# Attention values of the late steps as 64-by-64 products in three rounds, turning moved behind the scores, and each score minimum signalled by itself

## The chip, the cores and the metric

The kernel runs on one core of a Trainium2 chip. The metric is the device time of one execution in microseconds (us); less is better. The engines are named as in the profile: PE is TensorE (PEld its weight loads), DVE is VectorE, ACT is ScalarE, POOL is GpSimd, SP is SyncE, which here only issues DMAs. Each engine works through its own queue in order, and waits in it on semaphores.

## The reference, cut to what matters

One step of a two-layer decoder trunk on 1,024 prompt tokens and 8 sample tokens, 1,024 features wide, in fp32. Layer 0 is a gated linear recurrence. Layer 1 is attention with 16 query heads of 64 features and 2 key/value heads, over a window of 128 keys, with a learned sink for each head, and a SiLU gate on its output. The change touches the attention of the prompt alone:

```python
def _sink_attention(q, k, v, mask, sinks):
    s = jnp.einsum('bnqkgd,bnskd->bnkgqs', q, k) * scale      # blocks of 128 queries by 256 keys
    s = jnp.where(valid, s, MASK_VALUE)                       # 0 <= query - key <= 128
    m = jnp.maximum(jnp.max(s, axis=-1, keepdims=True), sink)
    p = jnp.where(valid, jnp.exp(s - m), 0.0)
    denom = jnp.sum(p, axis=-1, keepdims=True) + jnp.exp(sink - m)
    return jnp.einsum('bnkgqs,bnskd->bnqkgd', p / denom, v)
```

The result is multiplied by the gate and goes through a product with `w_out`, a residual add and a last RMS norm.

## The kernel before, in words

Weights and activations of the large products are cut into a high and a low part (fp32r), and each product is three passes (high by high, high by low, low by high); every such matmul streams 344 tokens. They fill PE for nearly the whole kernel. The attention is spread over that stream of matmuls as **steps**, `for s in range(-3, NQ)` with `NQ` = 32. Query group `q` (0 to 31) is four heads of one block of 128 queries: `q // 8` picks the heads, `q % 8` the block. Where `q % 8` is 0 there is no block of keys in front, and each piece of work for that q is half as large. In step s PE does, in this order:

- `values(s - 1)`: probabilities times values. It waits until both turned halves of the probabilities have been copied to SBUF (`pt_early` by ACT, `pt_late` by DVE) and until the output before it has been read (`gated`).
- `turn(s)`: transposes the probabilities of s into two PSUM banks, after POOL's `normalise(s)` (`p_done`). It signals `pt_done`.
- `scores(s + 2)`: queries by keys, in quarters of 64 features by 64 queries, after the minima of s + 1 have been read (`sc_read`). It signals `sc_done`.
- its share of the large products: 16 or 17 matmuls in a step (`gates_part`) up to s = 15, and 18 in a step (`output_part`) from s = 16 on. Output unit 0 of token segment i waits for `tile_lo` of that segment.

`two_banks(q)` is true for q from 11 (`Q_TWO`) on, other than q = 16 and 24: 19 of the 32 groups. There `values` uses two PSUM banks, `R[4]` for the first 64 queries and `G[2]` for the other 64, and leaves out the keys that the window masks: first four products of 128 keys by 64 features (the "far" ones), then four of 64 keys by 64 features (the "near" ones). For other q there are four products of 128 keys by 64 features over 256 columns, half as many where `q % 8` is 0. An fp32 matmul shows as two MATMUL records.

In step s DVE does `denominators(s + 1)` (waits for the exponentials of s + 1), `gate_output(s - 1)` (waits for `pv_done`), `copy_late(s)` (waits for `pt_done`), `minima(s + 2)` (four reductions from PSUM, waits for the scores and for `turn(s)`, whose buffer it writes), and then the **extra work** that the step has: evacuating gate units (`gate_raw2`, `gate_minimum`) or output units (`first_half`), low parts of weights (`prepare`, `prepare_half`), small pieces for the sample tokens, and in s = 15, 16, 17 the low part of a token segment (`AR`, "tile_lo"). ACT does `copy_early(s)`, from s = 17 on `cut_slice(s - 1)`, then high parts, the three functions of a gate's softplus, and last `exponentials(s + 2)`, which waits until all four minima have been taken. POOL does `normalise(s + 1)` after DVE's `denominators(s + 1)`.

Of the kernel before, what the change touches and what calls it, by code (L numbers as in the profile page):

```python
# [126 lines left out]
def output_fill(s):  # L127

    return 18 * max(0, s - 15)


GATE_END = [min(s for s in range(-3, NQ) if gates_fill(s) >= 24 * (g + 1)) for g in range(NU * (HP - BG_FIRST))]
OUT_END = [min(s for s in range(NQ) if output_fill(s) >= 12 * (g + 1)) for g in range(NU * KT)]
SLOT = (2, 3, 4, 5, 0, 1, 6, 7)


# [18 lines left out]
def build(nc, ctx, ins, outs):  # L155
# [234 lines left out]
    rd_done = sem("rd_done")  # L390
    p_done = sem("p_done")
    pt_done = sem("pt_done")
    pt_early = sem("pt_early")
    pt_late = sem("pt_late")
    pv_done = sem("pv_done")
# [26 lines left out]
    def seg(i):  # L422
        return slice(i * TU, (i + 1) * TU)
# [465 lines left out]
    def _(act):  # L889
# [276 lines left out]

        def exponentials(q):
            keys = slice(P if q % NC == 0 else 0, 2 * P)
            act.wait_ge(sc_read, 2 * q + 2)
            sm = small[:, q % 2]  # L1170
            for i in range(4):
                nc.scalar.activation(SP_[q % 2][:, i, keys], SP_[q % 2][:, i, keys], ACT.Exp, bias=sm[:, 0, i:i + 1],  # L1172
                                     scale=-1.0, accum_out=sm[:, 2, i:i + 1])
            act.wait_ge(m_ready, q + 1)
            nc.scalar.activation(sm[:, 3, :], sm[:, 1, :], ACT.Exp).then_inc(p_exp, 1)
# [15 lines left out]
        for s in range(-3, NQ + 1):  # L1191
            if 0 <= s < NQ:
                copy_early(s)
            if s >= 17:
                cut_slice(s - 1)
            for n in range(N_B2 + 2, N_BO):
                if end_step(n - 3) + 1 == s:
                    prepare(n)
            for h in range(2 * KT):
                if half_step(h) == s:  # L1200
                    prepare_half(h)
            if s == 5:
                act.wait_ge(d_max, 1)
                nc.scalar.activation(SSN[:], SSN[:], ACT.Exp, bias=dsm[:, 1:2], accum_out=dsm[:, 3:4])
                nc.scalar.activation(dsm[:, 4:5], dsm[:, 2:3], ACT.Exp).then_inc(d_exp, 1)
            if 15 <= s < 18:
                i = s - 15
                act.wait_ge(unit_done, NU * (N_BO - 1) + i + 1)
                act.wait_ge(gated, (11, 14, 16)[i])
                act.wait_ge(d_gated, 1)  # L1210
                nc.scalar.activation(XL[:, 0:HK, seg(i)], A[:, 0:HK, seg(i)], ACT.Copy).then_inc(tile_hi, 1)
            if s == 22:
                act.wait_ge(d_gated, 2)
                nc.scalar.activation(XL[:, HK:HP, SEQ:T], A[:, HK:HP, SEQ:T], ACT.Copy).then_inc(dec_hi, 1)
            for g in range(NU * (HP - BG_FIRST)):
                if GATE_END[g] + 2 == s:
                    gate_exponential(NU * BG_FIRST + g)
            for g in range(NU * (HP - BG_FIRST)):
                if GATE_END[g] + 1 == s:
                    gate_softplus(N_B2 + g // NU, g % NU)  # L1220
            if 0 <= s + 2 < NQ:
                exponentials(s + 2)
# [34 lines left out]
    def _(dve):  # L1257
# [384 lines left out]
        def minima(q):  # L1642

            keys = slice(P if q % NC == 0 else 0, 2 * P)
            sm = small[:, q % 2]
            h = 4 * (q // NC)
            if q >= 2:
                dve.wait_ge(pt_done, q - 1)
            for jj in range(2):
                dve.wait_ge(sc_done, 2 * q + 2)  # L1650
                for v in range(2):
                    i = 2 * jj + v
                    ps = R[v][:, 2 * P * jj:2 * P * (jj + 1)]
                    ins = nc.vector.tensor_tensor_reduce(  # L1654
                        out=SP_[q % 2][:, i, keys], in0=ps[:, keys], in1=amask[:, keys], scale=1.0,
                        scalar=sink[:, h + i:h + i + 1], op0=ALU.add, op1=ALU.min, accum_out=sm[:, 0, i:i + 1])
                ins.then_inc(sc_read, 1)
            dve.wait_ge(sc_read, 2 * q + 2)
            nc.vector.tensor_tensor(sm[:, 1, :], sm[:, 0, :], sink[:, h:h + 4], ALU.subtract).then_inc(m_ready, 1)

        def denominators(q):
# [51 lines left out]
        for s in range(-3, NQ + 1):  # L1713
            if 0 <= s + 1 < NQ:
                denominators(s + 1)
            if 0 <= s - 1:
                gate_output(s - 1)
            if 0 <= s < NQ:
                copy_late(s)
            if 0 <= s + 2 < NQ:  # L1720
                minima(s + 2)
            for g in range(NU * (HP - BG_FIRST)):
                if GATE_END[g] == s:
                    gate_raw2(N_B2 + g // NU, g % NU)
# [42 lines left out]
                                      ).then_inc(d_done, 1)  # L1767
            if s == 14:
                sample_gates(0, HK, 1)
            if 15 <= s < 18:  # L1770
                i = s - 15
                dve.wait_ge(tile_hi, i + 1)
                nc.vector.tensor_tensor(AR[:, 0:HK, seg(i)], A[:, 0:HK, seg(i)], XL[:, 0:HK, seg(i)].bitcast(fp32),  # L1773
                                        ALU.subtract).then_inc(tile_lo, 1)
            if s == 21:
                sample_gates(HK, HP, 2)
            if s == 22:
# [19 lines left out]
    def _(pe):  # L1797
# [280 lines left out]
        def scores(q):  # L2078
            p, nb = query(q)
            keys = slice(P if nb == 0 else 0, 2 * P)  # L2080
            tok = slice((nb - 1) * P + keys.start, (nb + 1) * P)
            if q:
                pe.wait_ge(sc_read, 2 * q)
            else:
                pe.wait_ge(q_rot, HP)
                pe.wait_ge(kb_done, 1)
            for jj in range(2):
                for v in range(2):
                    rows = slice(64 * v, 64 * v + 64)
                    if nb == 0:  # L2090
                        ins = nc.tensor.matmul(R[v][:, 2 * P * jj + P:2 * P * (jj + 1)], pair(A, q)[rows, jj],
                                               KNEG[rows, tok], start=True, stop=True)
                        continue
                    for u in range(0, P, 64):
                        ins = nc.tensor.matmul(R[v][u:u + 64, 2 * P * jj + u:2 * P * jj + u + 192],  # L2095
                                               pair(A, q)[rows, jj, u:u + 64],
                                               KNEG[rows, tok.start + u:tok.start + u + 192], start=True, stop=True)
                ins.then_inc(sc_done, 1)

        def turn(q):  # L2100
# [9 lines left out]
                                                  ident[rows, rows])  # L2110
            ins.then_inc(pt_done, 1)

        def values(q):
            p, nb = query(q)
            pe.wait_ge(pt_early, q + 1)
            pe.wait_ge(pt_late, q + 1)
            if q:
                pe.wait_ge(gated, q)
            blocks = key_blocks(q)
            if two_banks(q):  # L2120
                if q == Q_TWO:
                    pe.wait_ge(d_done, 1)
                for near in range(2):
                    for u in range(2):
                        kb = u ^ near
                        ks = slice(64 * kb ^ 64, (64 * kb ^ 64) + 64) if near else slice(0, P)
                        for v in range(2):
                            rows = slice(64 * v, 64 * v + 64)
                            ins = nc.tensor.matmul(  # L2129
                                (R[4], G[2])[u][rows, 0:P].rearrange("p (j w) -> p j w", j=2),  # L2130
                                VP[ks, nb - 1 + kb, rows],
                                turned(kb)[ks, :, v, u],
                                start=not near, stop=bool(near))
                ins.then_inc(pv_done, 1)
                return
            for kb in blocks:
                for v in range(2):
                    rows = slice(64 * v, 64 * v + 64)
                    ins = nc.tensor.matmul(R[4][rows, 0:2 * P].rearrange("p (j u w) -> p j u w", j=2, u=2),  # L2139
                                           VP[:, nb - 1 + kb, rows], turned(kb)[:, :, v], start=(kb == blocks[0]), stop=(kb == 1))  # L2140
            ins.then_inc(pv_done, 1)
# [44 lines left out]
        for s in range(-3, NQ):  # L2186
            if s >= 1:
                values(s - 1)
            if s >= 0:
                turn(s)  # L2190
            if s == 0:
                pe.wait_ge(vp_done, 2)
            if 0 <= s + 2 < NQ:
                scores(s + 2)
            if s < 16:
                gates_part(gates_fill(s - 1) if s > -3 else 0, gates_fill(s))
            else:
                output_part(output_fill(s - 1), output_fill(s))
# [17 lines left out]
            if s == 9:  # L2216
# [6 lines left out]
                                           stop=(b == DEC - 1))  # L2223
                ins.then_inc(d_out, 1)
        values(NQ - 1)
        pe.wait_ge(dec_lo, 1)
        for i, ready in enumerate((11, 14, 16)):
            pe.wait_ge(slice_lo, ready)
# [82 lines left out]
```

## Time and profile before

| | |
|---|---|
| time, median of 3 (lowest to highest) | 954.62 us (953.82 to 955.58) |
| the profiled execution: its own time / its span | 955.42 us / 953.5 us |
| PE busy | 942.5 us of the span, 99% |
| DVE / ACT / POOL busy | 608.2 / 409.9 / 396.3 us |
| steps of the attention | scores from 712 us on, last values at 896 us |
| DMA | 89.86 MB in all, 93 GB/s over the span |

The span is from the first to the last instruction of the profiled execution; the own time has some 1.9 us more around it. A record's start is exact enough to take the pace of an engine from the distance of two starts; the length of a matmul record holds its latency too, so that lengths of neighbouring records overlap.

### The profile page before, as it was taken

How to read it: one execution, taken by the hardware profiler on the slowest of the kernel's cores; microseconds unless marked ns; L12 is line 12 of the kernel's file. 1: busy time of each engine (PE TensorE's matmuls, PEld its weight loads, DVE VectorE, ACT ScalarE, POOL GpSimd, SP SyncE). 2: the span in 40 equal slices, each digit the busy share in tenths (PEclk: the TensorE clock that was granted, in tenths of full speed). 3: DMA queues.
4: the chain of work that ended last, by engine and by line, in shares of the span. 5: the costliest groups of instructions: out<-in, count | busy, mean ns of one | idle time of the engine just before them, and what ended most of it. 6: DMA issues, size and time to landing. Idle time of an engine off the chain costs nothing.

```text
span 953.5 us, 21616 instructions
## 1 busy us (share of the span) xinstructions
PE 942.5 (99%) x8948; PEld 895.0 (94%) x8948; DVE 608.2 (64%) x1220; ACT 409.9 (43%) x821; POOL 396.3 (42%) x295
## 2 busy tenths in 40 slices
PE   9999999999999999999999999999999999999996
PEld 9999999999999999899999999999998788788995
DVE  6596676767575666639733235466667877977634
ACT  7532424243434334434422233532127768766423
POOL 2383635445362734403234441451105534445343
PEclk9999999999999999999999999999999999999999
DMA  9422121313131304334033413221112223333104
GB/s 356 184 91 80 58 101 59 93 46 94 45 93 46 114 25 138 113 105 149 23 134 138 151 67 134 73 90 45 45 54 88 68 68 111 98 92 88 34 31 149
DMA packets 53202, 89.86 MB, mean 94 GB/s; under 512 B 15625, under 2 KB 35049, under 8 KB 52977
## 3 DMA queue, kind: packets, MB, share of 16 engines
q1 hardware_dynamic: 52672, 88.11, 27.7%
q8 instruction: 71, 1.16, 0.5%
q10 hardware_dynamic: 432, 0.37, 0.1%
q14 instruction: 27, 0.21, 0.1%
HBM read 70.83 MB, written 17.64 MB: 93 GB/s over the span
## 4 chain that ended last, share of the span: by engine, by line
PE 94%; DMA 2%; SPq 1%; ACT 1%; DVE 1%; issue 0%; POOL 0%; DVEq 0%; ACTq 0%
PE G L1820 66%; PE G L2164 9%; PE R L2095 2%; PE R L2109 2%; DMA ST<-xs 2%; PE R L1933 1%; PE R L1921 1%; PE R L2129 1%; PE R L1891 1%; PE R L1936 1%; PE R L1820 1%; PE R L2139 1%; PE R L1861 1%; PE R L1911 1%; SPq L547 1%; PE R L1873 1%
## 5 line engine op out<-in xcount | busy, mean ns | idle before, releaser
L1820 PE MATMUL G<-XH,WH 128*128 128x344 f32 x1152 | 370.5, 324 | 0.6 <-ACT XH L1021 0.6
L1820 PE MATMUL G<-XL,WH 128*128 128x344 f32 x1152 | 366.9, 321 | 0.0
L1820 PE MATMUL G<-XH,WL 128*128 128x344 f32 x744 | 234.0, 320 | 0.1
L1820 PEld LDWEIGHTS G<-XH,WH 128*128 128x128 f32 x1152 | 216.0, 188 | 7.7 <-issue 5.2
L1820 PEld LDWEIGHTS G<-XL,WH 128*128 128x128 f32 x1152 | 216.0, 188 | 2.5 <-issue 2.2
L741 POOL TENSOR_TENSOR WL<-WR,WH 128x1024 fp32r<-128x1024 f32 x40 | 107.5, 2687 | 188.7 <-ACT WH L908 162.1
L1820 PEld LDWEIGHTS G<-XH,WL 128*128 128x128 f32 x744 | 139.1, 188 | 0.4 <-POOL WL L741 0.4
L1820 PE MATMUL G<-XL,WL 128*128 128x344 f32 x408 | 130.7, 320 | 0.0
L840 POOL TENSOR_TENSOR SP<-SP,small 128x1024 f32<-128x1024 f32 (+1 forms) x32 | 57.2, 1789 | 115.4 <-DVE small L1665 115.4
L908 ACT ACTIVATE WH<-WR 128x1024 fp32r<-128x1024 f32 x56 | 59.0, 1055 | 57.3 <-PE G L1820 30.8
L779 POOL TENSOR_TENSOR K<-K,FP 128x512 f32<-128x512 f32 x48 | 61.3, 1277 | 48.5 <-PE R L1911 14.1
L1820 PEld LDWEIGHTS G<-XL,WL 128*128 128x128 f32 x408 | 76.7, 188 | 0.8 <-issue 0.6
L1172 ACT ACTIVATE SP<-SP,small 128x256 f32<-128x256 f32 (+1 forms) x128 | 61.7, 483 | 32.3 <-DVE small L1654 32.3
L735 POOL TENSOR_TENSOR WR<-WR,gain 128x1024 f32<-128x1024 f32 x18 | 37.0, 2064 | 60.2 <-DMA WR<-w 60.2
L1820 PE MATMUL G<-AR,WH 128*128 128x344 f32 x192 | 61.3, 319 | 0.0
L1820 PE MATMUL G<-GR,WH 128*128 128x344 f32 x192 | 61.3, 319 | 0.0
L1820 PE MATMUL G<-GR,WL 128*128 128x344 f32 x192 | 61.3, 319 | 0.0
L1654 DVE CUSTOM_DVE_ANT_0 SP<-R,amask,sink 128x256 f32<-128x256 f32 (+1 forms) x128 | 52.0, 462 | 3.7 <-PE R L2095 3.3
L2164 PE MATMUL G<-XL,WH 128*128 128x344 f32 x144 | 48.0, 333 | 0.4 <-DVE AR L1773 0.4
L2164 PE MATMUL G<-XL,WL 128*128 128x344 f32 x144 | 46.0, 319 | 0.0
L2164 PE MATMUL G<-AR,WH 128*128 128x344 f32 x144 | 45.9, 319 | 0.0
L1553 DVE TENSOR_TENSOR H<-G,RESO 128x344 f32<-128x344 f32 x24 | 12.3, 514 | 40.4 <-PE G L1820 40.2
(303 smaller groups left out, 1779.1 us busy)
## 6 DMA issues: line engine op xcount, KB each, us to landing
WR<-w SPq DMA_DIRECT2D x56, 512.0 KB, 3.9
A<-x SPq DMA_DIRECT2D x8, 516.0 KB, 7.7
FG<-head_scales SPq DMA_DIRECT2D x8, 516.0 KB, 3.7
RESO<-x SPq DMA_DIRECT2D x8, 516.0 KB, 4.6
h_spill<-H SPq DMA_DIRECT2D x8, 516.0 KB, 2.9
gate_spill<-EV SPq DMA_DIRECT2D x24, 172.0 KB, 1.9
RES<-h_spill SPq DMA_DIRECT2D x24, 172.0 KB, 2.6
SS<-states SPq DMA_DIRECT2D x8, 512.0 KB, 5.8
```

Source lines behind the costliest of these rows:

```text
L735: nc.gpsimd.tensor_tensor(WR[:, n % 3], WR[:, n % 3], gain[:, kind, :].unsqueeze(2).broadcast_to([P, KT, P]), ALU.mult).then_inc(gained, 1)
L741: nc.gpsimd.tensor_tensor(WL[:, n % 3], WR[:, n % 3], WH[:, n % 3].bitcast(fp32), ALU.subtract).then_inc(lo_pool, 1)
L779: nc.gpsimd.tensor_tensor(low, low, decay(l, 1).unsqueeze(2).broadcast_to([P, SEQ // (2 * h), h]), ALU.mult).then_inc(upd_k, 1)
L840: nc.gpsimd.tensor_tensor(sp_, sp_, small[:, q % 2, 4, :].unsqueeze(2).broadcast_to([P, 4, keys.stop - keys.start]), ALU.mult).then_inc(p_ ...
L908: nc.scalar.activation(WH[:, n % 3], WR[:, n % 3], ACT.Copy).then_inc(hi_done, 1)
L1172: nc.scalar.activation(SP_[q % 2][:, i, keys], SP_[q % 2][:, i, keys], ACT.Exp, bias=sm[:, 0, i:i + 1], scale=-1.0, accum_out=sm[:, 2, i:i ...
L1553: nc.vector.tensor_tensor(H1[:, m, seg(i)], G[i][:, 0:TU], RESO[m % 2][:, seg(i)], ALU.add).then_inc(unit_read, 1)
L1654: ins = nc.vector.tensor_tensor_reduce(out=SP_[q % 2][:, i, keys], in0=ps[:, keys], in1=amask[:, keys], scale=1.0, scalar=sink[:, h + i:h ...
L1820: return nc.tensor.matmul(U[unit_bank(NU * n + i)][:, 0:TU], w[:, n % 3, k, :], x[:, seg(i)], start=(k == 0 and p == 0), stop=(k == KT - 1 ...
L2095: ins = nc.tensor.matmul(R[v][u:u + 64, 2 * P * jj + u:2 * P * jj + u + 192], pair(A, q)[rows, jj, u:u + 64], KNEG[rows, tok.start + u:tok ...
L2109: ins = nc.tensor.transpose(R[2 + u][:, cols], SP_[q % 2][rows, i, kb * P:(kb + 1) * P], ident[rows, rows])
L2164: return nc.tensor.matmul(G[unit_bank(u)][:, 0:TU], wt[:, k, :], x, start=(w == 0), stop=(w == 11))
```

## The change

The values of a two-bank group become twelve products of 64 keys by 64 features in three rounds of four. Rounds 1 and 2 stand where `values` stood, the scores of s + 2 come next, then round 3 (`rest_values`), and `turn(s)` is last. Round 3 writes the two banks from the other half of the array's rows, and waits for the end of round 2 on a new semaphore, `pv_most`. The other groups keep their products, but `turn(s)` comes behind `scores(s + 2)` for them too. On DVE `minima(s + 2)` goes ahead of `copy_late(s)`. `sc_read` is raised by each of the four minima, and ACT takes each exponential after its own minimum. The three segment low parts (with ACT's high parts) go from steps 15, 16, 17 to 15, 18, 22, and on DVE to right behind `copy_late`.

```diff
+TILE_STEP = (15, 18, 22)
...
         def exponentials(q):
             keys = slice(P if q % NC == 0 else 0, 2 * P)
-            act.wait_ge(sc_read, 2 * q + 2)
             sm = small[:, q % 2]
             for i in range(4):
+                act.wait_ge(sc_read, 4 * q + i + 1)
                 nc.scalar.activation(SP_[q % 2][:, i, keys], SP_[q % 2][:, i, keys], ACT.Exp, bias=sm[:, 0, i:i + 1],
...
-            if 15 <= s < 18:
-                i = s - 15
+            if s in TILE_STEP:
+                i = TILE_STEP.index(s)
...
-                    ins = nc.vector.tensor_tensor_reduce(
+                    nc.vector.tensor_tensor_reduce(
...
-                ins.then_inc(sc_read, 1)
-            dve.wait_ge(sc_read, 2 * q + 2)
+                        ).then_inc(sc_read, 1)
+            dve.wait_ge(sc_read, 4 * q + 4)
...
+            if 0 <= s + 2 < NQ:
+                minima(s + 2)
             if 0 <= s < NQ:
                 copy_late(s)
-            if 0 <= s + 2 < NQ:
-                minima(s + 2)
+            if s in TILE_STEP:
+                i = TILE_STEP.index(s)
+                dve.wait_ge(tile_hi, i + 1)
+                nc.vector.tensor_tensor(AR[:, 0:HK, seg(i)], A[:, 0:HK, seg(i)], XL[:, 0:HK, seg(i)].bitcast(fp32),
+                                        ALU.subtract).then_inc(tile_lo, 1)
...
-            if 15 <= s < 18:
-                i = s - 15
-                dve.wait_ge(tile_hi, i + 1)
-                nc.vector.tensor_tensor(AR[:, 0:HK, seg(i)], A[:, 0:HK, seg(i)], XL[:, 0:HK, seg(i)].bitcast(fp32),
-                                        ALU.subtract).then_inc(tile_lo, 1)
...
-                pe.wait_ge(sc_read, 2 * q)
+                pe.wait_ge(sc_read, 4 * q)
...
+        def quarter_values(q, n, *parts):
+
+            nb = query(q)[1]
+            for u, (kb, kh) in enumerate(parts):
+                ks = slice(64 * kh, 64 * kh + 64)
+                for v in range(2):
+                    rows = slice(64 * v, 64 * v + 64)
+                    ins = nc.tensor.matmul((R[4], G[2])[u][rows, 0:P].rearrange("p (j w) -> p j w", j=2),
+                                           VP[ks, nb - 1 + kb, rows], turned(kb)[ks, :, v, u], start=(n == 0), stop=(n == 2))
+            return ins
+
+        def rest_values(q):
+
+            if two_banks(q):
+                pe.wait_ge(pv_most, sum(two_banks(v) for v in range(q + 1)))
+                quarter_values(q, 2, (0, 1), (1, 0)).then_inc(pv_done, 1)
...
             if two_banks(q):
                 if q == Q_TWO:
                     pe.wait_ge(d_done, 1)
-                for near in range(2):
-                    for u in range(2):
-                        kb = u ^ near
-                        ks = slice(64 * kb ^ 64, (64 * kb ^ 64) + 64) if near else slice(0, P)
-                        for v in range(2):
-                            rows = slice(64 * v, 64 * v + 64)
-                            ins = nc.tensor.matmul(
-                                (R[4], G[2])[u][rows, 0:P].rearrange("p (j w) -> p j w", j=2),
-                                VP[ks, nb - 1 + kb, rows],
-                                turned(kb)[ks, :, v, u],
-                                start=not near, stop=bool(near))
-                ins.then_inc(pv_done, 1)
+                quarter_values(q, 0, (0, 0), (0, 1))
+                quarter_values(q, 1, (1, 0), (1, 1)).then_inc(pv_most, 1)
                 return
...
             if s >= 1:
                 values(s - 1)
-            if s >= 0:
-                turn(s)
             if s == 0:
                 pe.wait_ge(vp_done, 2)
             if 0 <= s + 2 < NQ:
                 scores(s + 2)
+            if s >= 1:
+                rest_values(s - 1)
+            if s >= 0:
+                turn(s)
...
         values(NQ - 1)
+        rest_values(NQ - 1)
```

## Rows read from the trace of the kernel before

**Rows 1.** The page: the span, and each engine's busy time.

```profile
span 953.5 us, 21616 instructions
PE 942.5 (99%) x8948; PEld 895.0 (94%) x8948; DVE 608.2 (64%) x1220; ACT 409.9 (43%) x821; POOL 396.3 (42%) x295
```

**Rows 2.** Waits from 722 to 900 us: who waited, for whom, total, times, longest.

```profile
DVE small L1664 <- ACT small L1175: 24.4, 25, 1.6
...
PE R L2129 <- DVE PT L1673: 0.5, 1, 0.5
```

**Rows 3.** Timeline of PE in a late step: start, us, engine, line, tiles, shapes.

```profile
864.75 0.32 PE L2164 MATMUL G<-XL,WXL 128*128 128x344 f32 x1
865.00 0.44 PE L2129 MATMUL R<-PT,VP 128*64 128x128 f32 x4
...
865.59 0.33 PE L2129 MATMUL R<-PT,VP 64*64 64x128 f32 x2
...
865.97 0.72 PE L2109 MATMUL R<-ident,SP 64*128 64x64 f32 x16
866.62 0.88 PE L2095 MATMUL R<-KNEG,A 64*64 64x192 f32 x16
867.43 0.43 PE L2164 MATMUL G<-XL,WXH 128*128 128x344 f32 x1
```

**Rows 4.** Timeline of PE, a step whose turning is half as large.

```profile
855.68 0.46 PE L2109 MATMUL R<-ident,SP 64*128 64x64 f32 x8
...
856.07 0.88 PE L2095 MATMUL R<-KNEG,A 64*64 64x192 f32 x16
```

**Rows 5.** Timeline of DVE around a late step, and ACT's copy behind turning.

```profile
868.02 0.48 DVE L1654 CUSTOM_DVE_ANT_0 SP<-R,amask,sink 128x256 f32<-128x256 f32 x1
...
869.84 0.52 DVE L1694 TENSOR_TENSOR H<-G,RES 128x344 f32<-128x344 f32 x1
...
871.96 0.16 DVE L1664 TENSOR_TENSOR small<-small 128x4 f32<-128x4 f32 x1 [1.61 <-ACT small L1175]
872.07 0.88 PE L2095 MATMUL R<-KNEG,A 64*64 64x192 f32 x16
...
872.18 0.60 ACT L1183 ACTIVATE PT<-R 128x512 f32<-128x512 f32 x1 [0.25 <-PE R L2109]
...
872.25 0.27 DVE L1682 TENSOR_TENSOR A<-R,SGR 128x128 f32<-128x128 f32 x1
...
872.64 0.68 DVE L1673 COPY PT<-R 128x512 f32<-128x512 f32 x1
```

**Rows 6.** Timeline of DVE and PE in steps 16 to 18, with PE's two waits.

```profile
813.33 0.43 PE L2164 MATMUL G<-XL,WH 128*128 128x344 f32 x1 [0.43 <-DVE AR L1773]
...
817.63 1.29 DVE L1265 TENSOR_TENSOR WL<-WR,WH 128x512 fp32r<-128x512 f32 x2
...
819.26 1.58 DVE L1773 TENSOR_TENSOR AR<-A,XL 128x1376 fp32r<-128x1376 f32 x1
...
821.29 0.32 PE L2164 MATMUL G<-XL,WL 128*128 128x344 f32 x1
...
821.37 0.68 DVE L1673 COPY PT<-R 128x512 f32<-128x512 f32 x1
...
822.15 0.44 PE L2129 MATMUL R<-PT,VP 128*64 128x128 f32 x4 [0.55 <-DVE PT L1673]
```

**Rows 7.** Timeline of DVE's extra work in step 4.

```profile
749.67 1.22 DVE L1260 TENSOR_TENSOR WL<-WR,WH 128x1024 fp32r<-128x1024 f32 x1
...
751.91 0.15 DVE L1664 TENSOR_TENSOR small<-small 128x4 f32<-128x4 f32 x1
```

**Rows 8.** Timeline of ACT and DVE in step 12.

```profile
792.01 1.14 ACT L920 ACTIVATE WH<-WR 128x512 fp32r<-128x512 f32 x2
...
793.06 0.48 ACT L1150 ACTIVATE EV<-EV 128x344 f32<-128x344 f32 x1
...
795.00 0.52 DVE L1609 SCALAR_TENSOR_TENSOR EV<-EV,EV 128x344 f32<-128x344 f32 x1 [0.44 <-ACT EV L1146]
```

More of the change, by code:

```diff
@@ L392, in build @@
     pt_done = sem("pt_done")
+    pv_most = sem("pv_most")
     pt_early = sem("pt_early")
@@ L1653, in minima @@
                     ps = R[v][:, 2 * P * jj:2 * P * (jj + 1)]
-                    ins = nc.vector.tensor_tensor_reduce(
+                    nc.vector.tensor_tensor_reduce(
                         out=SP_[q % 2][:, i, keys], in0=ps[:, keys], in1=amask[:, keys], scale=1.0,
-                        scalar=sink[:, h + i:h + i + 1], op0=ALU.add, op1=ALU.min, accum_out=sm[:, 0, i:i + 1])
-                ins.then_inc(sc_read, 1)
-            dve.wait_ge(sc_read, 2 * q + 2)
+                        scalar=sink[:, h + i:h + i + 1], op0=ALU.add, op1=ALU.min, accum_out=sm[:, 0, i:i + 1]
+                        ).then_inc(sc_read, 1)
+            dve.wait_ge(sc_read, 4 * q + 4)
             nc.vector.tensor_tensor(sm[:, 1, :], sm[:, 0, :], sink[:, h:h + 4], ALU.subtract).then_inc(m_ready, 1)
```

## The prediction

> **What bounds the kernel now.** I read the page first: PE is busy for 942.5 of 953.5 us [rows 1], so only what shortens or lengthens PE's own queue counts. Next the waits from 722 to 900 us, the stretch of the steps [rows 2]: PE hardly waits (0.5 us once, for DVE's late copy; the timeline shows 0.43 us more for a segment low part [rows 6]). DVE waits 24.4 us for ACT's exponentials. That costs nothing as long as PE does not wait for DVE in turn. Then the timeline of one late step. It shows what PE's step is made of, and that the parts hold fixed time besides their streaming.
>
> **PE's late step before** [rows 3]. The first values record starts at 865.00, the near ones at 865.59, turning at 865.97, scores at 866.62, the large products at 867.43. So values take 0.97 us, turning 0.65 us, scores 0.81 us. How much of a part is fixed? Turning with 8 records takes 0.39 us [rows 4], with 16 it takes 0.65 us [rows 3]: 8 records cost 0.26 us, and about 0.14 to 0.16 us is left over. The other parts fit the same. A round of the near products is four at a time; if a fp32 record of 128 columns takes 0.107 us on each of four quarters (scores have 192 columns and 4 rounds: 4 x 0.16 = 0.64 us of their 0.81), the near block is 2 x 0.107 + 0.17 = 0.38 us, as measured. The far block runs two at a time: 4 x 0.107 + 0.16 = 0.59 us, as measured. I take 0.16 us for each change of the array's shape (128x64, 64x64, 64x128, 128x128), and 0.09 us from the large products into values (864.75 + 0.157 to 865.00).
>
> The Trainium skill (TensorEngine Tiling (Array Packing), Key Properties) says that changing the tiling mode, and not merely the tile, drains the array. It gives no time for it; the sum would be the same by it, and it is the reason why I tie the 0.16 us to the change of shape and not to each part.
>
> **What the new form saves on PE.** Streaming is equal: before 4 far rounds and 2 near ones (0.43 + 0.21 us), after 6 rounds of 0.107 us, 0.64 us. Changes of shape: before far, near, turning, scores, large; after values/scores/round 3 all in 64x64, then turning, then large. Far to near is gone in all 19 two-bank groups: 19 x 0.16 = 3.0 us. Turning to scores is gone where scores still follow, 16 times: 16 x 0.16 = 2.6 us. Together 5.6 us. In the other steps the order changes and the count of shapes does not: 0.
>
> **The wait for `pv_most`.** The end of a part reaches another engine about 0.27 us after its streaming ends: ACT's copy starts 0.11 us after the block behind turning (872.07 to 872.18 [rows 5]), plus the 0.16 us before that block. With 0.08 us to get going again this is 0.35 us. Scores stream for 0.64 us in between, so it is hidden 16 times. In steps 30, 31 and after the last one no scores stand there: 3 x 0.35 = 1.05 us lost. Bounds: 0 and 0.5 us each.
>
> The Trainium skill (TensorE: Matmul & The Clock Gate, "The cost: per-tile semaphore tail") gives 25 + 4.7 x 4 + 26.3 = 70 ns as the tail of one signal behind four tiles. By that, as an estimate, the three waits would cost 0.2 us in place of 1.05 us; no row here shows a PE wait for itself.
>
> **The new hand-off.** A late step after the change, from the start of values: rounds 1 and 2 end at 0.43, scores at 1.07, round 3 at 1.28, turning runs from 1.44 to 1.93, large products start at 2.09 and take 17 x 0.157 + 0.20 = 2.86 (18: 3.03), so the next values could start at 4.95 to 5.12. Now DVE: `minima` needs turning, which is now last, and gets its signal at 2.20. Four minima take 1.62 and with the small subtraction 1.82 us (868.02 to 869.84 [rows 5]); only then comes `copy_late`, 0.68 us long, and PE starts 0.10 us after its end (821.37 + 0.68 to 822.15 [rows 6]). Values can start at 2.20 + 1.82 + 0.78 = 4.80. That leaves 0.15 to 0.3 us. Before, the copy came ahead of the minima and had 2.4 us to spare in this stretch. In an early step (values 1.01, scores 0.81, turning 0.65) the signal is at 2.57, the copy through at 5.17 and values due at 5.33: 0.16 us.
>
> So from DVE's end of the copy (4.60) to the next turning signal (4.95 + 2.20) there are 2.55 us, of which denominators take 0.29 and the output 0.40 us (871.96 to 872.25 to 872.64 [rows 5]). Extra work above some 1.9 us, or anything that holds the denominators, pushes minima, copy and then PE. I went through the 32 steps with the durations of the rows. Five overflow:
> - **Step 4**: two gate records (0.85), a whole weight low part and the sample tokens' chain (749.67 to 751.91, 2.24 us [rows 7]) make 3.1 us, with a short wait for ACT 3.4; room with slack is 2.5. PE waits 1.0 us in step 5.
> - **Step 12**: ACT has its copy, two weight halves (1.05, start to start [rows 8]), the exponential and a softplus (1.56) behind turning: 2.20 + 0.49 + 1.05 + 0.37 + 1.56 + 0.15 = 5.8, that is 0.86 into the next step. There DVE's `gate_minimum` waits (it waited 0.44 before [rows 8]), then 0.42 + 1.2 for the two low halves, 0.69, minima at 3.58 in place of 2.20, values at 6.16 in place of 4.97: 1.2 us.
> - **Step 15**: ACT's high part of the segment (1.24) stands in the same queue; its exponentials end at 2.9 of step 16, minima start at 3.77, PE waits 1.2 us.
> - **Step 16**: 0.42 + two low halves 1.2 + 0.43, after 0.3 of waiting: 0.5 us. **Step 18**: segment low part 1.5 (its record is 1.58 long [rows 6]) + 0.6 + 0.43: 0.5 us.
>
> Sum 4.4 us. The same addition over step 17 of before gives a wait of 0.75 us where the rows show 0.61 (822.15 against 821.29 + 0.157 + 0.09 = 821.54, [rows 6]), so I take a tenth off: 4.0 us.
>
> **Waits that go.** The segment low parts of before cost PE 0.5 us in step 16 (`AR`; the large products started at 813.33 [rows 6] where scores of 0.81 us would have let them start at 812.83), 0.61 us in step 18, and 0.25 us of small waits around: 1.4 us back. The moved ones are due in steps 16, 21 and 26, so none is late. Each minimum signalled alone: ACT starts its exponentials 1.2 us sooner, and DVE waits less for them (1.61 us in that step [rows 5]). PE is not behind that wait, so 0 by itself; where ACT's queue is the late one (steps 12, 15) it starts at once either way. SyncE's load of the gate waits for `gated`, now 0.5 us later, for data needed two steps on: 0. POOL's normalising has a step to spare: 0.
>
> **Sum**: -5.6 + 1.05 + 4.0 - 1.4 = -1.95 us, taken as -1.9. The profiled span 953.5 would become 951.6; its own time 955.42 lies 0.8 us above the median shown; against the median 954.62 I predict **952.7 us**. Own range: all of the five stalls in full and 0.5 us each for the last waits give about -1.1; none of the last waits and half of the stalls -5.0; -3.6 to -0.3 is where I see it.
>
> **Rivals.**
> - **The stalls do not come** (the slack of 0.15 us is larger, ACT is ahead): -5.6 + 1.05 - 1.4 = -6.0, at least -4: 948.6 to 950.6. For it: DVE waits for ACT in 25 steps before [rows 2], so it has time. Against: that time lies ahead of the denominators, not between turning and the copy. 0.18.
> - **The hand-off binds in ordinary steps**: if signals take 0.3 us more than I add, some 24 ordinary steps wait 0.15 us each: +3.6 - 1.9 = +1.7, 956.3. It decides from 0.25 us on. The slack is that thin. 0.14.
> - **Quarter products are slower than 0.107 us a round** (the side where it gets slower): only 8 records in a row at 64x64 and 128 columns are seen [rows 3], and the fixed part cannot be told from the pace there. At the pace of the scores, 0.04 us a record, 24 records take 0.96 and not 0.64 us: 19 x 0.32 = +6.1, 958.8. The gain is gone once a record takes 0.031 us in place of 0.027. 0.12. The Trainium skill (TensorEngine Tiling (Array Packing), Instruction Overhead) puts about 60 cycles on every matmul, so that more and smaller ones win nothing; 128 columns are above that, so by it the pace would hold.
> - **The change of shape costs nothing by itself**: the 0.16 us is the fill of any new block; then little of the 5.6 us comes and the stalls stay: +1 to +3.7, 955.6 to 958.3. Against: the near block shows 0.17 with the same banks, operands and line as the far one. 0.08.
>
> **Chances and range.** My forecast 0.48, half of it beyond 0.2% (1.9 us, which is about what a measurement of this kernel can tell from no change), half within. Faster by over 0.2%: 0.24 + 0.18 = 0.42. Within: 0.24 + 0.07 (thin hand-off) + 0.02 = 0.33. Slower: 0.07 + 0.10 + 0.08 = 0.25. The range leaves out the ends of the first and the third rival: 949.0 to 957.0; that of the forecast alone is 951.0 to 954.3.
>
> **What would show it.** In the trace after: no gap between rounds 2 and scores, the late step from values to large products 2.1 us long (2.43 before) and 2.46 still in the early ones; DVE's minima starting 0.11 us behind the large products' first record; PE waiting for `PT` L1673 or its new line in steps 5, 13, 16, 17, 19, 0.5 to 1.2 us each, 4 us in sum; three short PE gaps ahead of round 3 at the end; no wait for `AR`. The prediction is wrong if values, scores and round 3 take over 1.4 us, or if PE waits for the late copy in most steps or in none.

## The result, and the profile after

The changed kernel takes 958.82 us (median of 6 runs, 957.07 to 960.0), beside 955.39 us for the kernel before (6 runs on the same chip, 953.82 to 955.88). The ratio is 1.0036 [1.0027, 1.0046]: 3.4 us slower, where 1.9 us faster was predicted. The profiled execution took 957.11 us.

The page of the kernel after, the lines that answer to [rows 1]:

```profile
span 955.2 us, 21920 instructions
PE 936.5 (98%) x9100; PEld 894.7 (94%) x9100; DVE 612.0 (64%) x1220; ACT 407.5 (43%) x821; POOL 397.6 (42%) x295
```

PE's busy time fell by 6.0 us (942.5 before) while the span grew by 1.7 us. So PE now waits some 8 us more than it did. The waits of the kernel after, from 722 to 902 us, those of PE and the ones that answer to [rows 2]:

```profile
PE R L2148 <- issue: 4.2, 3, 1.6
PE R L2122 <- issue: 3.6, 3, 1.7
...
DVE small L1666 <- ACT small L1177: 4.8, 8, 1.2
```

Six waits ahead of the values (L2122 the late form, L2148 the early one) make 7.8 us. The profile puts them down to "issue", that is to nothing it can name. DVE's wait for ACT's exponentials, 24.4 us before, is 4.8 us, and PE did not gain by it. Both the signals and the new order on DVE shorten it. Between e4 and h3 below, which differ in the signals alone, it falls from 25.5 to 7.8 us; in e3, with the new order and the old signals, it is 10.0 us.

An ordinary late step of the kernel after (to be held against [rows 3] and [rows 5]), PE, DVE and ACT:

```profile
867.51 0.33 PE L2122 MATMUL R<-PT,VP 64*64 64x128 f32 x2
...
867.68 0.28 PE L2122 MATMUL G<-PT,VP 64*64 64x128 f32 x2
...
867.79 0.28 PE L2122 MATMUL G<-PT,VP 64*64 64x128 f32 x2
...
868.00 0.83 PE L2097 MATMUL R<-KNEG,A 64*64 64x192 f32 x16
...
868.65 0.28 PE L2122 MATMUL G<-PT,VP 64*64 64x128 f32 x2
...
868.98 0.71 PE L2111 MATMUL R<-ident,SP 64*128 64x64 f32 x16
...
869.62 0.42 PE L2173 MATMUL G<-XL,WXH 128*128 128x344 f32 x1
...
869.73 0.49 DVE L1656 CUSTOM_DVE_ANT_0 SP<-R,amask,sink 128x256 f32<-128x256 f32 x1
...
871.47 0.17 DVE L1661 TENSOR_TENSOR small<-small,sink 128x4 f32<-128x4 f32 x1
871.56 0.69 DVE L1675 COPY PT<-R 128x512 f32<-128x512 f32 x1
...
872.65 0.33 PE L2122 MATMUL R<-PT,VP 64*64 64x128 f32 x2
```

This step is as drawn up. Values, scores and round 3 take 1.47 us and the large products start at 2.11 (2.09 predicted; 2.43 before). A round is 0.11 us apart from the next. Minima start 0.11 us behind the large products, and the copy ends at 872.25, 0.3 us before the next step would want it. The step is 5.14 us long and was 5.46 us.

The time is lost in six other steps. Length of a step in us, from one start of values to the next, read from PE's timeline of each kernel (e1, e2 and h2 are experiments, below):

| step | before | after | e1 | e2 | h2 |
|---|---|---|---|---|---|
| 3 | 5.46 | 6.67 | 5.45 | 5.45 | 5.45 |
| 5 | 5.33 | 6.85 | 5.93 | 5.33 | 6.30 |
| 10 | 6.79 | 5.34 | 6.79 | 6.80 | 5.39 |
| 13 | 5.29 | 6.72 | 5.87 | 4.98 | 6.17 |
| 14 | 4.98 | 5.12 | 5.14 | 5.36 | 5.14 |
| 16 | 5.69 | 6.64 | 5.78 | 5.04 | 6.10 |
| 17 | 5.80 | 5.62 | 5.40 | 5.42 | 5.63 |
| 18 | 5.48 | 5.13 | 5.12 | 5.36 | 5.12 |
| 19 | 5.44 | 6.77 | 6.78 | 6.49 | 6.03 |
| 20 | 5.60 | 5.14 | 5.12 | 5.44 | 5.12 |
| 22 | 5.13 | 5.29 | 5.29 | 5.29 | 5.30 |
| 26 | 5.46 | 5.14 | 5.14 | 5.14 | 5.14 |
| 30 | 4.64 | 4.81 | 4.81 | 4.80 | 4.81 |

Against the length that these steps have where nothing holds them (5.45, 5.33, 4.98, 4.96, 5.06, 5.13; in steps 16 and 17, which no kernel here shows free of waits, that is their own length less PE's wait at the end), the kernel after loses 1.2, 1.5, 1.7, 1.7, 0.6 and 1.6 us in steps 3, 5, 13, 16, 17 and 19: 8.3 us. The prediction had five of them, with 4.0 us.

**What holds the step.** The end of step 13 in the kernel after, timeline of POOL, DVE and PE:

```profile
800.94 0.91 POOL L836 TENSOR_TENSOR EV<-EV,EV 128x344 f32<-128x344 f32 x1
801.05 0.82 DVE L1661 TENSOR_TENSOR small<-small,sink 128x4 f32<-128x4 f32 x1
...
801.79 0.68 DVE L1675 COPY PT<-R 128x512 f32<-128x512 f32 x1
...
802.58 0.33 PE L2122 MATMUL R<-PT,VP 64*64 64x128 f32 x2 [1.66 <-issue]
```

The subtraction of 4 numbers in a partition is 0.82 us long, and ends 0.02 us behind POOL's gate product, which began just before it (800.94 + 0.91 = 801.85 against 801.87). The copy stands right behind, and PE behind the copy. The same pair at the end of step 2, where POOL multiplies by the gain:

```profile
742.63 1.90 POOL L737 TENSOR_TENSOR WR<-WR,gain 128x1024 f32<-128x1024 f32 x1
...
742.89 1.65 DVE L1661 TENSOR_TENSOR small<-small,sink 128x4 f32<-128x4 f32 x1
...
744.46 0.68 DVE L1675 COPY PT<-R 128x512 f32<-128x512 f32 x1
...
745.24 0.65 PE L2148 MATMUL R<-PT,VP 128*64 128x256 f32 x4 [1.15 <-issue]
```

742.63 + 1.90 = 744.53; 742.89 + 1.65 = 744.54. And the subtraction in all 30 steps of this stretch, shortest, median and longest record in ns:

```profile
L1661 DVE TENSOR_TENSOR small<-small,sink x30: 161/166/1651, 725.6 to 886.9; 128x4 f32<-128x4 f32 x30
```

The median is the price that the prediction used; nine records are from 0.6 to 1.65 us long. The kernel before has the same hold, in the same place:

```profile
742.44 1.90 POOL L735 TENSOR_TENSOR WR<-WR,gain 128x1024 f32<-128x1024 f32 x1
...
743.25 1.11 DVE L1659 TENSOR_TENSOR small<-small,sink 128x4 f32<-128x4 f32 x1
```

There the late copy had been done before the minima, so nobody on PE's side waited.

The profiles of before and after must not be subtracted without one more look. Windows of both kernels; the columns are the stretch, its length, busy time of PE, PEld, DVE, ACT and POOL with instructions, then the granted clock. First before, then after:

```profile
777.60:782.90 5.30, 5.30 (x50) 3.81 (x50) 2.78 (x11) 1.40 (x5) 2.81 (x2) 0.68 0.17 48
```

```profile
777.60:782.90 5.30, 5.30 (x62) 4.04 (x61) 3.22 (x10) 2.54 (x11) 3.20 (x3) 1.00 0.50 158
```

In the profiled execution of before the granted clock falls in step 10: it is 0.50 from 779.0 to 781.5 us (the 1.2 GHz level), and 1.00 (2.4 GHz) there in the kernel after. This costs 1.45 us (6.79 against 5.34 us). It happens in some executions and not in others. The profiles that have such a stretch show a granted clock of 0.995 or 0.996 over the whole execution, those without one 0.997 or 0.998. Of the 46 executions of the kernel before that ran beside the experiments, 19 are below 0.997 and take about 1.5 us more in the median than the other 27. So the comparisons by steps leave step 10 out: 1.7 + 1.45 + 0.2 (the stretch began 0.2 us earlier) gives the 3.4 us of the medians. The kernel after has two executions at 0.997 (957.07 us, and 957.11 us in the profiled one) and four at 0.994 or 0.995 (958.14 to 960.00 us); what the clock did in those four no trace shows.

### The profile page after: what moved, and what is told of

Read it like the earlier page. It is cut to its first block, busy times and chain, and to the rows that moved or that the text cites. A ratio compares the mean times of both kernels' runs of the same rounds, so it can differ in the third digit from the quotient of the medians.

```text
span 955.2 us, 21920 instructions
## 1 busy us (share of the span) xinstructions
PE 936.5 (98%) x9100; PEld 894.7 (94%) x9100; DVE 612.0 (64%) x1220; ACT 407.5 (43%) x821; POOL 397.6 (42%) x295
## 4 chain that ended last, share of the span: by engine, by line
PE 97%; issue 1%; DMA 1%; DVE 1%; ACT 0%; SPq 0%; DVEq 0%
PE G L1822 67%; PE G L2173 10%; PE R L1822 2%; PE R L2097 2%; PE R L2111 2%; PE R L1935 1%; PE R L1923 1%; PE R L1893 1%; PE R L2122 1%; PE R L1938 1%; PE R L2148 1%; PE R L1863 1%; PE R L1913 1%; DMA A<-x 1%; PE R L1875 1%
## 5 line engine op out<-in xcount | busy, mean ns | idle before, releaser
L1185 ACT ACTIVATE PT<-R 128x512 f32<-128x512 f32 (+1 forms) x32 | 18.2, 569 | 52.7 <-PE R L2111 52.7
```

Of the source, the lines that this page charges most:

```text
L1185: nc.scalar.activation(PT[:, 0, keys], R[2][:, keys], ACT.Copy).then_inc(pt_early, 1)
```

## The experiments

**e1: the subtraction behind the copy.** The kernel after, with the subtraction a function of its own.

```diff
+        def sink_distance(q):
+            sm = small[:, q % 2]
+            h = 4 * (q // NC)
             dve.wait_ge(sc_read, 4 * q + 4)
             nc.vector.tensor_tensor(sm[:, 1, :], sm[:, 0, :], sink[:, h:h + 4], ALU.subtract).then_inc(m_ready, 1)
...
             if 0 <= s < NQ:
                 copy_late(s)
+            if 0 <= s + 2 < NQ:
+                sink_distance(s + 2)
```

> The changed kernel with DVE's small subtraction (minimum less sink) behind the late copy instead of ahead of it. Theory A (the subtraction is held until the GpSimd instruction in flight ends, and the late copy behind it is held with it): the copy is no longer held, PE's waits in steps 3, 5, 13, 16, 19 shrink from 7.8 us to about 3.8 us, the kernel gets 4 to 5 us faster than the changed one and lands 1 to 3 us under before. Theory B (the waits come from the amount of DVE work behind turning alone): only the 0.1 us of the subtraction itself leaves each waiting step, 0.6 us in all, so it stays 2.5 us or more over before.

Measured: 954.15 us (11 runs), ratio to before 0.9994 [0.9985, 1.0003], that is 4.0 us less than the kernel after by the two ratios. One instruction of 0.16 us, moved behind one of 0.68 us, gives back more than the whole loss. At the end of step 2 it is held as before, now harmlessly (e1's DVE timeline):

```profile
743.43 0.69 DVE L1679 COPY PT<-R 128x512 f32<-128x512 f32 x1
744.03 1.17 DVE L1665 TENSOR_TENSOR small<-small,sink 128x4 f32<-128x4 f32 x1
```

The copy, which reads PSUM, runs its 0.69 us through while POOL is in the same product (743.29 to 745.19). What stays in steps 5, 13, 16, 17 and 19 is 0.6, 0.9, 0.8, 0.3 and 1.7 us: 4.3 us, close to the 4.4 us of the prediction's walk. So the walk was right in sum for a DVE without the hold, and the hold is the 4 us on top.

**e2: the copy ahead of the minima.** The kernel after with the order on DVE that the kernel before had.

```diff
-            if 0 <= s + 2 < NQ:
-                minima(s + 2)
             if 0 <= s < NQ:
                 copy_late(s)
+            if 0 <= s + 2 < NQ:
+                minima(s + 2)
```

> The changed kernel with the late copy ahead of the minima on DVE, as before; everything else of the change kept. Both A and B say that the copy is then early enough everywhere: the waits for it go, the scores wait for the minima instead in three or four steps (1.0 to 1.5 us), the small three waits at the end stay (0.5 us by what the changed kernel showed). 4 to 5.5 us under before. Theory C (the smaller products and the new order on PE are themselves slower than the trace of one execution says): it stays within 1 us of before or over it.

Measured: 952.76 us (9 runs), 0.9973 [0.9964, 0.9983]: 2.6 us faster than before, 6.0 us faster than after. The stalls of steps 3, 5, 13 and 16 are gone with no other edit, so turning as the last part did not need the minima first. In steps 14, 18 and 20 it is now the scores that wait, 0.2 to 0.3 us, for a minimum of the group before. Step 17 has 0.36 us of waiting, 0.1 of it ahead of the scores and the rest among the large products. One stall stays, step 19. e2's timeline, where the segment's low part of the change (L1727) stands behind ACT:

```profile
825.49 0.63 ACT L922 ACTIVATE WXH<-WR 128x512 fp32r<-128x512 f32 x1 [1.77 <-DMA gate_spill<-EV]
...
826.03 1.33 ACT L1213 ACTIVATE XL<-A 128x1376 fp32r<-128x1376 f32 x1
...
827.40 1.59 DVE L1727 TENSOR_TENSOR AR<-A,XL 128x1376 fp32r<-128x1376 f32 x1 [2.08 <-ACT XL L1213]
...
828.90 0.69 DVE L1267 TENSOR_TENSOR WXL<-WR,WXH 128x512 fp32r<-128x512 f32 x1
829.51 0.51 DVE L1696 TENSOR_TENSOR H<-G,RES 128x344 f32<-128x344 f32 x1
...
830.16 0.40 PE L2173 MATMUL G<-XL,WH 128*128 128x344 f32 x1 [1.12 <-DVE H L1696]
```

Read backwards: PE waits for a bank that DVE reads into H; DVE is late from the low part; the low part waited 2.08 us for ACT's high part, which stood behind a half of the weights, which waited 1.77 us for the stored gates. In step 18 the segment meets this wait.

**e3: the kernel before with the minima ahead of the copy.** Only this order is changed.

```diff
-            if 0 <= s < NQ:
-                copy_late(s)
             if 0 <= s + 2 < NQ:
                 minima(s + 2)
+            if 0 <= s < NQ:
+                copy_late(s)
```

> The kernel before with one edit: minima ahead of the late copy on DVE. PE's products and order are as before. If the order of the two on DVE is what costs (A and B), this alone makes the kernel before 4 to 7 us slower, by waits of values for the late copy in steps 3, 5, 13, 16, 17, 18. If the cost of the change lies elsewhere, it stays within 1 us of before.

Measured: 961.10 us (5 runs), 1.0069 [1.0055, 1.0083]: 6.6 us slower. Steps 3 and 5 stall (6.26 and 6.82 us), and steps 17 and 18 grow to 8.15 and 6.98 us. Step 17 ends with a wait for the late copy. Step 18 has no such wait; its 1.5 us are the clock. e3's timeline of PE, the first values and the scores of step 18:

```profile
826.59 0.44 PE L2129 MATMUL R<-PT,VP 128*64 128x128 f32 x4 [2.92 <-DVE PT L1673]
...
828.21 1.56 PE L2095 MATMUL R<-KNEG,A 64*64 64x192 f32 x16
```

The same scores take 0.88 us in [rows 3]; the granted clock is 0.50 from 828.5 to 831.5 us. All five executions of e3 are below 0.997, so its loss against executions of before with a reduced clock is 5.4 us. The order alone, with none of the new products, still loses more than the whole change does.

**e4: the new products on PE alone.** The kernel before with `quarter_values`, `rest_values`, `pv_most` and PE's new order, DVE and ACT as they were.

```diff
-            if s >= 0:
-                turn(s)
             if 0 <= s + 2 < NQ:
                 scores(s + 2)
+            if s >= 1:
+                rest_values(s - 1)
+            if s >= 0:
+                turn(s)
```

> The kernel before with PE's part of the change alone: quarter products in three rounds around the scores, turning last; DVE's order, the signals of the minima and the steps of the segment low parts as before. The late step gets 0.32 us shorter 16 times (5.1 us), the end 0.5 us longer; the scores now ask for the minima 1.1 us earlier and the segment low parts of steps 15 to 17 still stand behind one another, so scores and the first output units wait for 2 to 3 us. 1 to 3 us under before. If turning last costs by itself, it is over before.

Measured: 953.39 us (11 runs), 0.9992 [0.9983, 1.0001]. Steps 16, 17 and 18 are 5.99, 6.28 and 6.26 us: the segments' low parts, crowded in three steps running, cost about 3.4 us there. Ordinary late steps are 5.14 us as after.

**h1: e2 with the middle segment in step 20.** `TILE_STEP = (15, 20, 22)` in place of (15, 18, 22).

> As e2_copy_first, with the second segment low part (and ACT's high part) in step 20 instead of 18. Theory A2 (in steps 18 and 19 the low part waits on DVE behind ACT's weight half, which waits for the stored gates, and holds the output evacuation and the minima behind it): the 1.37 us that PE loses in step 19 of e2_copy_first go, 1 to 1.4 us faster than e2_copy_first, 3.5 to 4 us under before. Rival (the loss comes from the amount of work of those steps): it moves to step 20 or 21 and the time stays within 0.4 us of e2_copy_first.

Measured: 951.26 us (5 runs), 0.9962 [0.9949, 0.9974]. Steps 19 and 20 are 5.14 and 5.12 us (6.49 and 5.44 in e2). So it was the place of the segment that cost step 19, not its length. In h1's timeline ACT still waits for the stored gates ahead of the same half of the weights (1.14 us), and PE does not wait behind it in steps 19 and 20.

**h2: POOL's long instructions cut in four.** The kernel after, with the gate product, the slice's low part and the product with the gain each issued as four instructions on a quarter. DVE is untouched.

```diff
-            nc.gpsimd.tensor_tensor(EV2[:, seg(i)], EV2[:, seg(i)], EV[:, seg(i)], ALU.mult).then_inc(gate_silu, 1)
+            for c in range(4):
+                part = slice(i * TU + 86 * c, i * TU + 86 * c + 86)
+                ins = nc.gpsimd.tensor_tensor(EV2[:, part], EV2[:, part], EV[:, part], ALU.mult)
+            ins.then_inc(gate_silu, 1)
```

> The changed kernel, DVE's order untouched, with three kinds of GpSimd instruction of the steps (gate product, low part of a slice, gain of a weight) each cut into four. Theory A (DVE's small subtraction is held until the GpSimd instruction in flight ends): its records get short (0.2 to 0.5 us where they were 0.6 to 1.65), PE's waits in steps 3, 5, 13, 16 shrink by 0.4 to 1.2 us each, 2 to 3.5 us faster than the changed kernel. If the subtraction is held for another reason (its own wait for the minima, ACT), the records keep their 0.6 to 1.65 us and the time stays.

Measured: 955.64 us (11 runs), 1.0012 [1.0003, 1.0021], 2.3 us less than after by the ratios and 3.5 us less by the steps of the profiles. Nothing on DVE or PE was edited, and the subtraction's longest record falls from 1651 to 367 ns. h2's rows, the subtraction in 30 steps and then the end of step 2:

```profile
L1669 DVE TENSOR_TENSOR small<-small,sink x30: 161/164/367, 725.8 to 883.6; 128x4 f32<-128x4 f32 x30
```

```profile
742.88 2.33 POOL L739 TENSOR_TENSOR WR<-WR,gain 128x256 f32<-128x256 f32 x4
...
743.22 0.29 DVE L1669 TENSOR_TENSOR small<-small,sink 128x4 f32<-128x4 f32 x1
```

It gets in between two of POOL's quarters, and no longer waits for the end of 1.90 us. This is what tells the hold by an instruction of POOL from a DVE that is only short of time. The quarters aren't free: the four take 2.33 us where one took 1.90. The steps of its profile put h2 level with before, 1.2 us under what the ratio says. The clock accounts for the difference: 9 of h2's 11 executions are below 0.997, of before only 10 of 21, so the two medians stand for different clocks. Like with like, h2 is 0.1 to 0.2 us over before (table below).

**h3: e2 without the spreading.** The low parts in steps 15, 16 and 17 at their old place.

> As e2_copy_first, but with the three segment low parts in steps 15, 16, 17 at their old place at the end of DVE's step. Against e2_copy_first it prices the spreading, against e4_pe_alone the signals of the minima. By the rows of e4_pe_alone, where steps 16, 17, 18 take 5.99, 6.28 and 6.26 us against 5.04, 5.42 and 5.36 in e2_copy_first (2.7 us in all, of which the spreading gives 1.4 us back in step 19), 1 to 1.5 us slower than e2_copy_first; within 0.5 us of e4_pe_alone if the signals are worth little.

Measured: 953.43 us (11 runs), 0.9989 [0.9981, 0.9998]. It differs from e4 in nothing but the single signals of the minima, and their ratios agree within 0.0003: these signals are worth nothing that can be measured. Against e2 the spreading is worth 1.5 us by the ratios, though the intervals touch; steps 16 to 18 are 6.01, 6.27 and 6.26 us again.

**h4: the best of these.** h1, and the last three groups in the old far and near form.

```diff
+                if q + 3 < NQ:
+                    quarter_values(q, 0, (0, 0), (0, 1))
+                    quarter_values(q, 1, (1, 0), (1, 1)).then_inc(pv_most, 1)
+                    return
+                for near in range(2):
+                    ...
```

> As h1_segment_at_20, and the last three groups, behind whose second round no scores stand, in the old form of far and near products. In the changed kernel they took 1.13 us in place of 0.97 us each. 0.5 us faster than h1_segment_at_20; 4 to 4.5 us under before if A2 holds.

Measured: 949.32 us (5 runs, 948.95 to 949.76), 0.9946 [0.9934, 0.9959]: 5.2 us faster than before and 8.6 us faster than after by the ratios. All five executions are at 0.997 or more; against such executions of before it is 4.7 us faster. Steps 30 and 31 are 4.64 us again. It beats both kernels.

The steps account for the times. For each kernel: the length from the values of step 1 to the end of the last ones less that of before, step 10 at its full-clock length in both, beside the ratio less 1, times 954.5 us. The last column compares medians of executions with a like granted clock, at 0.997 or more and below it; the groups are small (2 to 16 executions), and a dash stands where a kernel has none:

| kernel | by its steps | measured | interval | like clock (0.997 or more / below) |
|---|---|---|---|---|
| after | +3.4 | +3.4 | +2.6 to +4.4 | +2.9 / +4.3 |
| e1 | -0.7 | -0.6 | -1.4 to +0.3 | -0.5 / -1.1 |
| e2 | -2.4 | -2.6 | -3.4 to -1.6 | -3.0 / -2.9 |
| e3 | +7.0 | +6.6 | +5.2 to +7.9 | – / +5.4 |
| e4 | -0.8 | -0.8 | -1.6 to +0.1 | -1.0 / -1.0 |
| h1 | -4.1 | -3.6 | -4.9 to -2.5 | -4.1 / -4.1 |
| h2 | -0.1 | +1.1 | +0.3 to +2.0 | +0.1 / +0.2 |
| h3 | -1.0 | -1.1 | -1.8 to -0.2 | -0.9 / -0.9 |
| h4 | -4.5 | -5.2 | -6.3 to -3.9 | -4.7 / – |

For the kernel after, the granted clock of the six executions of before beside it is not on record; they are split by their time (953.82 and 954.62, the others 955.38 to 955.88). Only h2 falls outside its interval, and not at a like clock. The +7.0 of e3 holds the 1.5 us of reduced clock in its step 18; without them it is +5.5.

## Why the prediction was wrong, point by point

**The step that failed** is the price of the hand-off: "Four minima take 1.62 and with the small subtraction 1.82 us; only then comes `copy_late`". The 0.18 us of the subtraction came from an ordinary step [rows 5]. The subtraction waits for the POOL instruction in flight, up to 1.65 us, and the change puts the copy for PE behind it. e1 and h2 take the hold away from two sides, DVE's order and POOL's lengths, and both bring the time back (4.0 us, and 2.3 by the ratios or 3.5 by the steps); step 3, which the walk over the steps did not have at all, returns to 5.45 us in both. The kernel before had a record 1.11 us long at 743.25, so a look at shortest and longest records of each instruction that comes between turning and the copy would have shown it. The Trainium skill (SBUF — State Buffer, 🔬 SBUF: two separate sides) says that a DVE operation with two SBUF inputs and a GpSimd operation that reads SBUF take a shared pair of ports as an exclusive lock for a whole instruction. The trace agrees: the held subtractions end 0.02 us behind POOL's instruction, two that start 0.05 and 0.14 us ahead of POOL's gate product take 0.16 us, and the copy from PSUM isn't held.

**The saving on PE** was sized for 19 and 16 changes of shape, -5.6 + 1.05 = -4.55 us with the last waits. Fourteen late steps are 0.32 us shorter, as predicted. Two are not: in steps 14 and 22 the scores are those of a head's first group, whose shape is 64x128. Before and after, from PE's timeline of step 22:

```profile
845.09 0.71 PE L2109 MATMUL R<-ident,SP 64*128 64x64 f32 x16
845.64 0.66 PE L2091 MATMUL R<-KNEG,A 64*128 64x128 f32 x8
```

```profile
847.51 0.28 PE L2122 MATMUL R<-PT,VP 64*64 64x128 f32 x2
...
847.73 0.72 PE L2093 MATMUL R<-KNEG,A 64*128 64x128 f32 x8
848.38 0.33 PE L2122 MATMUL R<-PT,VP 64*64 64x128 f32 x2
...
848.76 0.71 PE L2111 MATMUL R<-ident,SP 64*128 64x64 f32 x16
```

Turning and these scores were one shape, so that nothing was to be saved between them; now they stand between two blocks of 64x64 and add a change. Steps 14 and 22 are 0.15 us longer. The saving is 14 x 0.32 - 2 x 0.15 - 3 x 0.17 = 3.7 us in place of 4.55: the count "16 times" was wrong, the 0.16 us was right. The rival that a change of shape costs nothing fell, and the one of slower quarters too (a round every 0.107 us).

**The wait for `pv_most`**, 0.35 us each against 0.16 saved, was to lengthen the last three by 0.19 us. They are 0.17 us longer; h4 takes it back. The 0.35 us held 0.08 us "to get going again" that no row gave, so that part of the agreement is luck. The Trainium skill (TensorE: Matmul & The Clock Gate, "The cost: per-tile semaphore tail"), with the 70 ns that its formula gives as an estimate, would have made these steps shorter than before. The measurement says otherwise: 0.17 us longer with 0.16 us saved is about 0.33 us for a wait.

**The five stalls** came in the steps named. Without the hold (e1) they are 0.6, 0.9, 0.8, 0.3 and 1.7 us where 1.0, 1.2, 1.2, 0.5 and 0.5 stood. That the sum is right is luck in part: four are 0.2 to 0.4 us too high, and step 19 is 1.2 us too low. "Step 18: segment low part 1.5 + 0.6 + 0.43: 0.5 us" was mis-sized by 1.2 us, because it left out that in the new place ACT's high part is itself behind the stored gates (e2's chain; h1 shows that the stall goes with the place, and no run takes ACT's wait away alone).

**The waits that go** came to 1.3 us (0.4, 0.7 and 0.2 in steps 16, 17 and 20) of 1.4. **Each minimum signalled alone** cost and gave nothing, as said (h3 against e4).

**Rivals.** The hand-off did not bind in ordinary steps: they are 5.12 to 5.14 us, and the slack of 0.3 us held. The rival of slower quarters had a time of 958.8 us, just what was measured; the rounds at 0.107 us show that this is chance. The true case, an instruction on the path whose length depends on another engine, was in none of them. In sum: -3.7 + 8.3 - 1.3 = +3.3 us where -1.9 was predicted; of the 5.2 us between, 4.0 are the hold, 0.9 the two steps with the other shape, and 0.3 the other stalls (4.3 against 4.0). Of its signs, "values, scores and round 3 take over 1.4 us" would read as met (turning starts at 1.47 us), but its own sum had turning at 1.44: the bound left out the change of shape ahead of turning.

Not tried: POOL's instructions kept away from the subtraction's time by waits, and a subtraction whose operand lies in PSUM. What starts the stretch of reduced clock in some executions and not in others is open.

## What to carry to other kernels

Before an instruction is put on the path, read its longest record as well as its median, and what ran on the other engines when it was long; a thin slack (here 0.3 us) is no place for one that another engine can hold. Where two jobs on an engine become free together, the one PE waits for goes first, and what only ACT or POOL wait for goes behind: here this one order was worth 6 us and decided the sign of the change. When a saving is counted as "so many changes of shape", list the shapes of every step, the exceptional ones too.

## What the hardware showed that was not expected

- A subtraction on 4 numbers in a partition, with two operands in SBUF, is held until POOL's instruction ends: 0.6 to 1.65 us in place of 0.16, in 9 of 30 steps. The profile counts the hold as DVE's busy time, so that no view of waits names it, and PE's wait behind it as "issue" (which e1's waits show too, so the word is no sign of the hold); with POOL's work in quarters the longest is 0.37 us.
- Step 10 takes 5.34 us in some executions and 6.79 in others, with a granted clock of 0.68 over 5.3 us. It comes right behind sixteen small products of 16 columns (before's timeline of PE):

```profile
775.77 1.96 PE L2222 MATMUL G<-PST,RES 128*128 128x16 f32 x16
777.66 1.20 PE L2139 MATMUL R<-PT,VP 128*64 128x256 f32 x8
```

  These are there in every kernel and every execution; the longer step is in the profiles of before, e1, e2, e4, h1 and h3 and not in those of after, e3, h2 and h4. In e3's profile the clock falls in step 18 instead, behind 2.92 us in which PE waited. It is 1.45 us, nearly as much as the difference of two profiled spans here.
